# Rows of lambda powers stored and loaded from GpSimd's queue, one group at a time, and two output blocks stored from ScalarE's queue

## What is computed

```python
proj = x @ w_in
q, k, v, u, g_att, g_ssm = split(proj)
y_att = neighbourhood_attention(q, k, v, rpb) @ w_na_out
lam_bar = exp(lam * dt)                      # 2 directions x 64 groups x 64 states, complex
bu = b_bar * u                               # b_bar = (lam_bar - 1) / lam * b
states[t] = lam_bar * states[t-1] + bu[t]    # forwards, and backwards for direction 1
y_s = Re(c * states) of both directions + d * u
y_s = gelu(y_s); y_s = y_s * sigmoid(y_s @ w_glu + b_glu)
mix = (sigmoid(g_att) * y_att + sigmoid(g_ssm) * (y_s @ w_s5_out)) @ w_out
h = LN(alpha * x + mix)
out = LN(alpha * h + (silu(h @ w_gate) * (h @ w_up)) @ w_down)
```

## Time and profile before

| | before |
|---|---|
| median of three runs | 1401.08 us |
| the profiled execution's own time | 1401.64 us |
| its span, from the first to the last instruction | 1399.8 us |
| busy: TensorE 1378.1 us, weight loads 1184.0, VectorE 948.8, ScalarE 689.1, GpSimd 82.9 | 98%, 85%, 68%, 49%, 6% of the span |
| granted clock of TensorE, mean | 0.997 |
| moved by DMA | 273.44 MB, 195 GB/s |
| lines of DMA issues that the change touches | `lrow<-lam_dram` x48, `lam_dram<-lamT` x6, `out<-hp` x9 |

### The profile page before, as it was taken

The page is one execution under the profiler, slowest core; times in us unless marked ns, Lnnn a source line. Parts: engine busy times, 40 slices in busy tenths (PEclk is TensorE's granted clock), DMA queues, the critical chain, the costliest instruction groups (busy, mean ns, idle before and its releaser), DMA issues.

```text
span 1399.8 us, 23670 instructions
## 1 busy us (share of the span) xinstructions
PE 1378.1 (98%) x9116; PEld 1184.0 (85%) x9116; DVE 948.8 (68%) x1297; ACT 689.1 (49%) x978; POOL 82.9 (6%) x88
## 2 busy tenths in 40 slices
PE   8998999999999999999999999999999999999998
PEld 7877888888888888887888888888888888888886
DVE  7977999999985789567555555555555554545454
ACT  5443555555456775336554445444554543333332
POOL 1800000000000000000122220000000000000001
PEclk9999999999999999999999999999999999999999
DMA  8767666666655686663666666666766666666663
GB/s 296 213 195 229 207 204 204 184 213 214 185 159 167 196 273 223 195 194 114 203 186 190 185 189 189 185 189 186 229 184 190 186 193 194 189 193 194 192 196 105
DMA packets 92402, 273.44 MB, mean 195 GB/s; under 512 B 14242, under 2 KB 25250, under 8 KB 91940
## 3 DMA queue, kind: packets, MB, share of 16 engines
q1 hardware_dynamic: 88788, 268.99, 62.0%
q10 hardware_dynamic: 3536, 3.38, 0.7%
HBM read 267.01 MB, written 5.31 MB: 195 GB/s over the span
## 4 chain that ended last, share of the span: by engine, by line
PE 90%; DVE 5%; DMA 2%; SPq 1%; issue 1%; ACT 0%; DVEq 0%; ACTq 0%
PE bank L1601 41%; PE bank L1603 21%; PE bank L1615 8%; PE bank L1616 8%; PE bank L1617 8%; DVE wlo L972 2%; PE bank L1713 1%; PE bank L1691 1%; DMA lrow<-lam_dram 1%; DMA raw<-wstream 1%; DVE scratch L998 1%; DVE scratch L995 1%; PE bank L1671 1%; PE bank L1891 0%; SPq L340 0%
## 5 line engine op out<-in xcount | busy, mean ns | idle before, releaser
L972 DVE TENSOR_TENSOR wlo<-raw,whi 128x1024 fp32r<-128x1024 f32 x463 | 567.2, 1225 | 318.4 <-ACT whi L569 314.8
L569 ACT ACTIVATE whi<-raw 128x1024 fp32r<-128x1024 f32 x463 | 489.4, 1059 | 472.4 <-PE bank L1603 246.6
L1601 PE MATMUL bank<-act,whi 128*128 128x512 f32 x2304 | 585.2, 395 | 10.3 <-DVE wlo L972 7.0
L1601 PEld LDWEIGHTS bank<-act,whi 128*128 128x128 f32 x2304 | 414.2, 189 | 90.7 <-DVE wlo L972 6.9
L1603 PEld LDWEIGHTS bank<-act,wlo 128*128 128x128 f32 x2304 | 314.6, 190 | 22.8
L1603 PE MATMUL bank<-act,wlo 128*128 128x256 f32 x2304 | 321.3, 282 | 0.0
L1615 PE MATMUL bank<-whi,mid 128*128 128x512 f32 x352 | 136.9, 389 | 0.0
L1616 PE MATMUL bank<-wlo,mid 128*128 128x512 f32 x352 | 136.9, 389 | 0.0
L1617 PE MATMUL bank<-whi,mid 128*128 128x512 f32 x352 | 136.9, 389 | 0.0
L1615 PE MATMUL bank<-whi,act 128*128 128x512 f32 x192 | 75.8, 395 | 3.4 <-DVE wlo L972 3.4
L1617 PEld LDWEIGHTS bank<-whi,mid 128*128 128x128 f32 x352 | 66.1, 188 | 13.8
(11 more groups left out here) (180 smaller groups left out, 1067.4 us busy)
## 6 DMA issues: line engine op xcount, KB each, us to landing
raw<-wstream SPq DMA_DIRECT2D x463, 512.0 KB, 3.7
bt<-b_rows SPq DMA_DIRECT2D x8, 512.0 KB, 5.7
lrow<-lam_dram SPq DMA_DIRECT2D x48, 64.0 KB
lnrow<-lnrows SPq DMA_DIRECT2D x3, 1024.0 KB, 6.8
xraw<-xT SPq DMA_DIRECT2D x8, 256.0 KB, 5.6
bs<-b_states SPq DMA_DIRECT2D x8, 256.0 KB, 5.2
tb<-lag_dram SPq DMA_DIRECT2D x32, 64.0 KB, 3.5
hp<-xtok SPq DMA_DIRECT2D x4, 512.0 KB, 4.6
```

Source lines behind the costliest of these rows:

```text
L569: act.activation(whi[:, c % SPL, :], raw[:, c % RAW, :], ACT.Copy).then_inc(hi_ready, 1)
L972: dve.tensor_tensor(wlo[:, c % SPL, :], raw[:, c % RAW, :], whi[:, c % SPL, :].bitcast(F32), ALU.subtract).then_inc(lo_ready, 1)
L1601: pe.matmul(bank[:, :], whi[:, s, i * P:(i + 1) * P], both, start=start and i == 0, stop=stop and i == kn - 1)
```

## The change

The six stores of the powers and all loads of rows leave SyncE's instruction list and go into GpSimd's, behind its tables. The rows are now loaded one group half at a time: destination 16 partitions, source the shape [16, 512] with the repeat outermost, so 12 DMAs of 32 KB for an eighth in place of six of 64 KB. VectorE's wait counts 192 for each eighth in place of 96. Those for eighth f are all issued at once when `bp_prod` says that eighth f - 1 has been read. In the tail SyncE stores VectorE's six blocks alone, in their order, and ScalarE's queue stores GpSimd's two.

```diff
-LN2_STORES = [0, 3, 1, 2, 7, 4, 5, 6]
...
-            def stage_rows(f, k):
-
-                d, j, n = ROWS_N[k]
-                row = lam_dram[n - 1, 2 * f + d, :, :, :].rearrange("g (o q) n -> g o (q n)", o=1)
-                sp.dma_start(lrow[j::Q, d, :, :, :].rearrange("p q r n -> p (q r n)"),
-                             row.to_broadcast([2, GC, 512])).then_inc(lrow_staged, 16)
-
-            def store_lam(n):
-
-                sp.wait_ge(lam_kept, 2)
...
-                if c in (24, 25, 26):
-                    store_lam(c - 23)
-                if c == 28:
-                    sp.wait_ge(rows_set, 2)
-                    sp.wait_ge(lam_stored, 96)
-                if c in (28, 29):
-                    for k in range(3 * (c - 28), 3 * (c - 28) + 3):
-                        stage_rows(0, k)
...
-                    if f == 0 and j in (1, 2):
-                        for k in range(3 * (j - 1), 3 * j):
-                            stage_rows(1, k)
...
-                    if 5 <= j < 11 and f + 2 < KS:
-                        stage_rows(f + 2, j - 5)
...
-            for i in LN2_STORES:
-                if i in LN2_DVE:
-                    sp.wait_ge(ln2_dve, LN2_DVE.index(i) + 1)
-                else:
-                    sp.wait_ge(ln2_pool, LN2_POOL.index(i) + 1)
+            for n, i in enumerate(LN2_DVE):
+                sp.wait_ge(ln2_dve, n + 1)
...
+            def stage_rows(f):
+
+                for d, j, n in ROWS_N:
+                    for g in range(2):
+                        row = lam_dram[n - 1, 2 * f + d, g:g + 1, :, :].rearrange("o q n -> o (q n)")
+                        pool.dma_start(lrow[64 * g + j:64 * g + 64:Q, d, :, :, :].rearrange("p q r n -> p (q r n)"),
+                                       row.to_broadcast([GC, 512])).then_inc(lrow_staged, 16)
+
+            pool.wait_ge(lam_kept, 2)
+            for n in range(1, Q):
+                o = (n - 1) % 2 * GROUPS
+                for g in range(2):
+                    pool.dma_start(lam_dram[n - 1, :, g, :, :],
+                                   lamT[o:o + GROUPS, (n - 1) // 2, g, :, :].rearrange("p r n -> p (r n)")).then_inc(lam_stored, 16)
+            pool.wait_ge(rows_set, 2)
+            pool.wait_ge(lam_stored, 96)
+            stage_rows(0)
+            for f in range(1, KS):
+                pool.wait_ge(bp_prod, 2 * f)
+                stage_rows(f)
...
+            for n, i in enumerate(LN2_POOL):
+                t, b = i // 4, slice(i % 4 * 512, i % 4 * 512 + 512)
+                act.wait_ge(ln2_pool, n + 1)
+                act.dma_start(out[t * P:(t + 1) * P, b], hp[:, t, b]).then_inc(pool_stored, 16)
...
-                    dve.wait_ge(lrow_staged, 96 * f + 96)
+                    dve.wait_ge(lrow_staged, 192 * f + 192)
```

More of the change, by code:

```diff
@@ L243, in build @@
             sem(n) for n in ("ln2_turned", "mrow_ready", "ln2_row", "ones_ready", "warm_ready"))
-        mrow_zero = sem("mrow_zero")
+        mrow_zero, pool_stored = sem("mrow_zero"), sem("pool_stored")
         ln2_dve, ln2_pool, stored = sem("ln2_dve"), sem("ln2_pool"), sem("stored")
@@ L468, in _ @@
             sp.dma_start(out[t * P:(t + 1) * P, b], hp[:, t, b]).then_inc(stored, 16)
-            sp.wait_ge(stored, 16 * len(LN2_STORES) + 16)
+            sp.wait_ge(stored, 16 * len(LN2_DVE) + 16)
+            sp.wait_ge(pool_stored, 16 * len(LN2_POOL))
         @block.gpsimd
```

## The result

The changed kernel takes **1392.95 us** (four runs, 1391.42 to 1393.46) against 1401.12 for the kernel before beside it (four runs, 1400.88 to 1401.36): ratio 0.994, 95% interval 0.9923 to 0.9957, 8.2 us faster. The forecast of 1402.8 us, no change or a little slower, went the wrong way. The time lies inside the outer range of 1389 to 1410 and outside the forecast's own 1398 to 1407; it falls between the two rivals A (1389.3) and A2 (1394), under A's condition for c.

What follows compares the result with a forecast made beforehand. TensorE, busy for 98% of the span, was taken as the bound; at c = 1.0 rows +2.6 us and tail -0.9 gave +1.7, from the median of 1401.08 to 1402.8 us; own range 1398 to 1407, outer 1389 to 1410.

Steps and rivals of the forecast that it cites:

- A: Rival: GpSimd's queue is quick, c at or under 0.64, both TensorE waits go, 11.8 us faster, 1389.3 us; chance 0.16.
- A2: Rival: c between 0.65 and 0.85, the waits shrink, about 1394 us; chance 0.18.
- c: Price of one DMA issue on GpSimd, not in the trace: taken as 1.0 us, with 0.5 and 2.4 as ends.
- The bound and the place: TensorE bounds; before the tail only its waits and slower clock from 92 to 134 us can matter, 10.9 us at most.
- Two engines for the rows, sixteen for the new shape: Old row loads use 2 DMA engines, new ones 16; the quicker landing saves some 8 us twice.
- the sum: Eighth 1's rows land at 84.53 + 30c; TensorE's chunk 33 moves by 2.6 + 30 (c - 1); the tail gives -0.9 us.
- Landing, 2.9 us after the issue's end: Time from issue's end to landing on GpSimd's queue: 2.9 us for row loads, 2.7 for stores.
- When the rows must be there: No TensorE wait if eighth 0's rows land by 93.2 us and eighth 1's by 103.6.
- The tail, -0.9 us: At the end SyncE's last store can issue 1.37 us earlier; 0.9 us gained, bounds 0 to 1.4.
- Later rounds and SyncE's freed issues: Later row loads, 12 us of a 41.4 us round, stay hidden; SyncE's 54 fewer issues of about 0.5 us gain nothing.

Runs made afterwards that it cites:

- experiment 7: The changed kernel with a second row buffer and its own semaphore for eighth 1, loaded without waiting for `bp_prod`: 1388.93 us against 1401.2 for the kernel before.
- Experiment 1: The kernel before with only the row loads' shape changed, 12 DMAs of 32 KB for an eighth, all still on SyncE: 1394.9 us against 1400.84.
- Experiment 2: The changed kernel with the old row shape put back, six loads of [2, 16, 512] for an eighth on GpSimd: 1401.42 us against 1400.84 for the kernel before.
- experiment 9: The changed kernel with a memset ahead of each row load of eighths 1 and 3 (128 columns) and 4 (512 columns): 1396.44 us against 1401.04.
- experiment 3: The kernel before with only the tail's new order of stores, two blocks from ScalarE's queue: 1400.16 us against 1400.84.
- experiment 4: The changed kernel with the old tail, all nine output stores on SyncE: 1394.43 us against 1400.84 for the kernel before.
- experiments 5 and 6: The changed kernel with a waited-for memset ahead of GpSimd's first 30 DMAs, 512 and 128 columns: 1409.63 and 1401.54 us against 1401.2 for the kernel before.

## Why the prediction was wrong, point by point

**The bound and the place: right.** All of the gain but the tail's lies in the stretch named, and 10.9 us was about its size: by TensorE's starts the changed kernel takes 8.0 of it and experiment 7 takes 10.9 with 1.0 us of wait left, so the most that it could give was some 1 us more.

**Two engines for the rows, sixteen for the new shape: right.** Experiment 1 shows it, with nothing changed but the shape and with it the number of loads: row packets two at a time before, up to 16 at a time after, and 5.9 us of gain. The rule of the Trainium skill (DMA: Bandwidth & Descriptors, Why a DMA increments its semaphore by 16 and not by 1), of which the trace before had only one half, is borne out in the other half too: the new shape has up to 16 packets in flight and no landing of 10 us. Experiment 2 is no second proof of it, since there GpSimd's stops make the time.

**GpSimd's issues, c = 1.0 us: the step that failed.** It is 0.483. The prediction took a dearer issue since "something of GpSimd's own has to make the descriptors", and leaned on rows of GpSimd's arithmetic, of which some took 1.3 us beside VectorE. These say nothing of a DMA issue. The nearest row in kind was SyncE's issue of the old load of the same rows, 0.520 in the median, within 8% of what came. It stood in the text as the lower end. With c = 0.5 the sum would have given the full gain and 1389.3. What the Trainium skill (DMA: Bandwidth & Descriptors, Specifications) gives, and by which the sum was read as the one at c = 1.0, is a time to the first byte and not the price of an issue; no run here shows a GpSimd queue that is slower by that ratio. The reading was off in itself, too: 0.52 us times 1 to 0.6 is 0.87, at which the sum is 2.6 - 3.9 - 0.9 = -2.2 us and not +1.7. As a switch of sign c did what the sum said: 0.48 gives -8.2, 1.0 gives +0.3, 1.33 gives +8.4 us.

**Landing, 2.9 us after the issue's end: too small at this pitch.** For the stores 2.7 was taken and 3.74 measured (GpSimd's idle time ahead of 79.51); for eighth 1's rows it was 6.17 - 0.48 = 5.7 after the issue's end. The sum at c = 0.48 puts those rows at 84.53 + 14.5 = 99.0; VectorE takes them up at 103.11. 2.8 us of the 4.1 are this landing. 1.2 stood ahead of it: GpSimd began eighth 1's loads at 91.54 where the sum has 90.3, since VectorE read eighth 0's rows at 88.90, right behind a split, and not at 87.7. The text had named an error of 1 us in it as one that would make the forecast wrong. It is the larger part of why the result is 8.2 and not the 11.8 of rival A; experiment 7, which takes that landing off the path, gives 12.3. The rows it was taken from the earlier trace rows were loads in fours and stores in pairs, not twelve in a row.

**When the rows must be there: half right.** TensorE's readiness for chunk 33 without the first wait was put at 107.3; in experiment 9 it stood from 112.51 - 5.25 = 107.26. But "by 103.6 no wait" was too kind: at 103.11 TensorE still lost 3.3 us in four waits, since VectorE, too, had stood and was behind with its splits.

**The tail, -0.9 us: about right.** It measured 0.7 (experiment 3) and 1.5 (changed kernel against experiment 4) by the times and 1.0 to 1.3 by the profiles. The last store goes at once behind VectorE's last half block, by SyncE's and VectorE's timelines:

```profile
1385.61 0.48 DVE L1579 SCALAR_TENSOR_TENSOR hp<-hp,lnm,bank 128x256 f32<-128x256 f32 x1
...
1386.11 0.47 SPq L436 DMA_DIRECT2D out<-hp  x1
```

That is 0.02 us behind it, where it was 1.43.

**Later rounds and SyncE's freed issues, worth nothing: right.** The round from 134 us is as full as before, with GpSimd's pause of 7 us in front of it and with memsets between the loads (experiment 9). The move to another queue on top of the shape bought 0.5 us at the most likely; this is what the Trainium skill says (DMA: Bandwidth & Descriptors, Issuing engines are not separate DMA queues), of a gain in issue time alone. Without the shape it bought nothing (experiment 2), but there the stops stand against it.

## What to carry to other kernels

A broadcast load whose outermost size is 2, issued from SyncE, was slow for itself and for every load beside it here: look for a landing of 10 us for 64 KB and for neighbours that slow down with it, and put the long dimension outermost before moving anything to another queue. For a price that the trace doesn't have, take the row of the same kind on another engine, not another kind of row on the same engine; and where the sign hangs on one price, say so and keep its nearer end likely. Where a buffer is reused at once and its load lies on the path, a second buffer for that one use can be worth more than a faster load.

## What the runs showed of the hardware that I had not expected

- A DMA issue of 32 KB (16 rows of 2 KB) takes 0.483 us on GpSimd, under SyncE's 0.589 for the same load; the first store, GpSimd's first DMA, took 0.72.
- GpSimd stops issuing after every 31 row loads with 1024 bytes of descriptor scratch, for 3.9 to 7.0 us in the changed kernel and experiment 9, and after 63 with 2048 bytes (3.6 us). It happened where the rows had time and cost nothing. With the old shape it came after every three loads, until the third had landed, and among eighth 1's it stood on the path (experiment 2).
- Two DMAs of the old shape are not alike on the two queues: on SyncE's the packets of six loads ran two at a time, on GpSimd's those of three loads up to six or seven at a time.
- Twelve loads of 32 KB in a row, in the changed kernel, land 2.2 to 3.9 us after their issue in eighth 0 and 4.1 to 6.2 in eighth 1. At a pitch of 1.0 or 1.33 us with TensorE standing (experiments 5 and 6) the medians are 2.4 to 3.7 us and the last of twelve lands in 1.8 to 2.0; in experiment 9 eighth 1's last takes 3.3.
